# Solving 8 by 8 blocks by substitution on VectorE in the delta rule's triangular inverses

## What is computed

```python
a_mat = jnp.where(strict, jnp.einsum('bnhid,bnhjd->bnhij', kb, kc) * decay, 0.0)
unit_lower = a_mat + jnp.eye(C, dtype=a_mat.dtype)
solve = functools.partial(lax.linalg.triangular_solve, left_side=True, lower=True, unit_diagonal=True)
u = solve(unit_lower, vb)
w = solve(unit_lower, kb * jnp.exp(gc)[..., None])
qk = jnp.where(lower, jnp.einsum('bnhid,bnhjd->bnhij', qc, kc) * decay, 0.0)
```

## Time and profile before

| | |
|---|---|
| median of 3 runs | 2768.18 us (2764.29 to 2771.28) |
| the profiled execution | 2771.26 us |
| its span | 2769.4 us |
| TensorE busy | 2725.2 us, 98% |
| VectorE busy | 1542.8 us, 56% |
| ScalarE busy | 1312.0 us, 47% |
| GpSimd busy | 119.9 us, 4% |
| delta rule's four groups | 360.7 to 466.0 us |

### The profile page before, as it was taken

The page is one execution under the profiler, slowest core; times in us unless marked ns, Lnnn a source line. Parts: engine busy times, 40 slices in busy tenths (PEclk is TensorE's granted clock), DMA queues, the critical chain, the costliest instruction groups (busy, mean ns, idle before and its releaser), DMA issues.

```text
span 2769.4 us, 44546 instructions
## 1 busy us (share of the span) xinstructions
PE 2725.2 (98%) x18174; PEld 2393.0 (86%) x18174; DVE 1542.8 (56%) x2048; ACT 1312.0 (47%) x1798; POOL 119.9 (4%) x167
## 2 busy tenths in 40 slices
PE   8999999999999999999999999999999999999999
PEld 8999998888888888888898997888888888888887
DVE  5655466666555555555544665666665555455454
ACT  4544444555544535445444354335555444354453
POOL 0000043000000000000000000530000000000000
PEclk9999999999999999999999999999999999999999
DMA  7454500543555555555545562004445545555553
GB/s 281 181 184 159 182 33 32 213 172 143 184 201 184 190 191 189 190 183 186 193 175 201 188 220 95 2 2 160 175 140 195 192 173 197 183 191 191 183 194 140
DMA packets 67801, 461.71 MB, mean 167 GB/s; under 512 B 7023, under 2 KB 10223, under 8 KB 13084
## 3 DMA queue, kind: packets, MB, share of 16 engines
q1 hardware_dynamic: 63824, 449.47, 45.3%
q10 hardware_dynamic: 3500, 5.21, 0.6%
q0 software_dynamic: 288, 4.19, 0.4%
HBM read 456.73 MB, written 5.27 MB: 167 GB/s over the span
## 4 chain that ended last, share of the span: by engine, by line
PE 94%; DVE 3%; ACT 2%; issue 1%; DMA 0%; POOL 0%; DVEq 0%; ACTq 0%; POOLq 0%
PE bank L423 17%; PE bank L402 13%; PE bank L404 13%; PE bank L403 13%; PE bank L425 9%; PE bank L446 6%; PE bank L448 6%; PE bank L447 6%; PE bank L1199 1%; PE bank L1172 1%; PE bank L337 1%; PE bank L2477 1%; PE bank L561 0%; PE bank L505 0%; DVE split_lo L353 0%
## 5 line engine op out<-in xcount | busy, mean ns | idle before, releaser
L353 DVE TENSOR_TENSOR split_lo<-raw,split_hi 128x1024 fp32r<-128x1024 f32 x840 | 1019.9, 1224 | 943.1 <-ACT split_hi L346 942.7
L346 ACT ACTIVATE split_hi<-raw 128x1024 fp32r<-128x1024 f32 x840 | 881.4, 1059 | 1137.6 <-PE bank L404 554.9
L423 PE MATMUL bank<-hT,split_hi 128*128 128x512 f32 x2048 | 720.8, 397 | 5.4 <-issue 5.3
L425 PE MATMUL bank<-hT,split_lo 128*128 128x256 f32 x2048 | 574.4, 280 | 0.0
L423 PEld LDWEIGHTS bank<-hT,split_hi 128*128 128x128 f32 x2048 | 385.0, 188 | 93.4 <-DVE split_lo L353 1.1
L402 PE MATMUL bank<-split_hi,u_hi 128*128 128x512 f32 x1152 | 449.8, 390 | 0.0
L404 PE MATMUL bank<-split_hi,u_lo 128*128 128x512 f32 x1152 | 448.5, 389 | 0.0
L403 PE MATMUL bank<-split_lo,u_hi 128*128 128x512 f32 x1152 | 448.4, 389 | 0.0
L425 PEld LDWEIGHTS bank<-hT,split_lo 128*128 128x128 f32 x2048 | 387.4, 189 | 5.7 <-issue 5.6
L446 PE MATMUL bank<-hT,split_hi 128*128 128x256 f32 x1328 | 376.8, 284 | 0.0
L448 PE MATMUL bank<-hT,split_lo 128*128 128x256 f32 x1328 | 375.8, 283 | 0.0
(11 more groups left out here) (471 smaller groups left out, 2266.4 us busy)
## 6 DMA issues: line engine op xcount, KB each, us to landing
raw<-in_stream SPq DMA_DIRECT2D x420, 1024.0 KB, 4.8
work<-in_mem POOLq DMA_DIRECT2D x2, 2048.0 KB, 8.5
bias_rows<-bias_line SPq DMA_DIRECT2D x1, 3072.0 KB, 12.9
x<-in_x SPq DMA_DIRECT2D x1, 2048.0 KB, 9.0
out<-x SPq DMA_DIRECT2D x4, 512.0 KB, 4.9
mwork<-bias_rows ACTq DMA_DIRECT2D x1, 1536.0 KB, 11.2
work<-bias_rows ACTq DMA_DIRECT2D x1, 1536.0 KB, 10.1
rwork<-in_wide ACTq DMA_DIRECT2D x1, 1280.0 KB, 5.9
```

What stands on the lines that cost most here:

```text
L346: nc.scalar.activation(split_hi[:, u % SPLIT], raw[:, b % RAW, (u % 2) * UNIT:(u % 2 + 1) * UNIT], ACT.Copy).then_inc(s_hi, 1)
L353: nc.vector.tensor_tensor(split_lo[:, u % SPLIT], raw[:, b % RAW, (u % 2) * UNIT:(u % 2 + 1) * UNIT], f32(split_hi[:, u % SPLIT]), SUB).th ...
L423: nc.tensor.matmul(out[:, :], lhsT=w_hi[:, cols], rhs=hT[:, k].rearrange("p two s -> p (two s)"), start=k == 0, stop=False)
L425: m = nc.tensor.matmul(out[:, S:2 * S], lhsT=w_lo[:, cols], rhs=hT_hi[:, k, :], start=False, stop=k == KD - 1)
```

## The change

A constant BASE = 3 and TINY = 8. The groups 0 to 3 (delta rule) start at level 3; RWKV's groups at level 1 as before. What stands for levels 0 to 2:

- VectorE, for each direction (dve_inv_blocks): multiply iv_diag with a mask of 8x8 blocks, sum over the blocks to 8 columns, spread these over the unit vectors.
- TensorE (pe_inv_around): one f32 product of 128x512 with a constant matrix, which puts all 8 rows of a block on each of its partitions, in bank 6 (bank 4 for group 0).
- VectorE, both directions together (dve_inv_solve): forward substitution for 8 systems in each partition, two operations a step in six steps after a first one, each waiting for the one before; then for each direction a product that spreads the result to blocks, and a transpose.

The tables DN_PE, DN_ACT and DN_DVE are new: cum, mask and kk of direction a are now made two groups ahead, in the last slot of a group (for group 1 before group 0), blocks and solve of the next group stand in slots 2 and 3 of VectorE. The fillers of slots 20 and 23 go; 14 stand in slots 4 and 8 of group 0 each, 8 in slot 15 of groups 2 and 3. Squares of the output move from VectorE to ScalarE, except for the last group. GpSimd makes three masks a group and direction instead of six; the masks of the low levels are loaded apart, on ScalarE's queue, for RWKV alone.

The diff, cut to its core:

```diff
@@
         def pe_inv_level(pe, group, views, AT, level, between):
             T, Tt, Pm, MT, _ = views
             for d in range(2):
-                pe.wait_ge(iv_t, nth(group, level - 1, d))
+                if level == base_of(group):
+                    pe.wait_ge(iv_tt, iv_tt_first(group, d))
+                    if group % 4:
+                        pe.wait_ge(iv_t, nth(group - 1, MASKS, d))
+                else:
+                    pe.wait_ge(iv_t, nth(group, level - 1, d))
...
+        def dve_inv_blocks(dve, group, views, d):
+
+            T, Tt = views[0][:, d], views[1][:, d]
+            if group >= 2 and d == 0:
+                dve.wait_ge(iv_f, group - 1)
+            dve.wait_ge(iv_a, 2 * group + d + 1)
+            own = const[:, C["blocks"]].unsqueeze(1).broadcast_to([P, 4, HALF])
+            dve_step(nc.vector.tensor_tensor(Tt, iv_diag[:, d], own, MULT))
+            dve_step(nc.vector.reduce_sum(tiny[:, 0, d], blocks_of(Tt).rearrange("p m b c -> p m c b"), AX_X))
...
+            nc.vector.tensor_tensor(blocks_of(T), got.broadcast_to(shape), unit.broadcast_to(shape), MULT).then_inc(iv_blk, 1)
+
+        def pe_inv_around(pe, group, views):
+
+            pe.wait_ge(iv_blk, 2 * group + 2)
+            pe.wait_ge(s_eg, 2 * group + 2)
+            nc.tensor.matmul(rep_bank(group)[:, :], lhsT=const[:, C["around"]],
+                             rhs=views[0].rearrange("p d m n -> p (d m n)"), start=True, stop=True).then_inc(iv_rep, 1)
+
+        def dve_inv_solve(dve, group, views):
...
+            dve.wait_ge(iv_rep, group + 1)
+            nc.vector.tensor_copy(row[:, :, 0:1], unit[:, :, 0:1])
+            dve_step(nc.vector.scalar_tensor_tensor(out=row[:, :, 1:], in0=N[:, :, 0, 1:], scalar=const[:, C["unit_neg"]],
+                                                    in1=unit[:, :, 1:], op0=MULT, op1=ADD))
+            for k in range(1, TINY - 1):
+                left = TINY - 1 - k
+                dve_step(nc.vector.tensor_tensor(part[:, :, 0:left], N[:, :, k, k + 1:],
+                                                 row[:, :, k:k + 1].broadcast_to([P, 8, left]), MULT))
+                dve_step(nc.vector.tensor_tensor(row[:, :, k + 1:], row[:, :, k + 1:], part[:, :, 0:left], SUB))
+            own = const[:, C["blocks"]].rearrange("p (b c) -> p b c", c=TINY).unsqueeze(1).broadcast_to([P, 4, TINY, TINY])
+            flat = lambda v: v.rearrange("p m s -> p (m s)")
+            for d, (solved, turned) in enumerate(((Tt, T), (T, Tt))):
+                nc.vector.tensor_tensor(blocks_of(solved[:, d]), own, tiny[:, 1, d].unsqueeze(2).broadcast_to([P, 4, TINY, TINY]),
+                                        MULT).then_inc(iv_tt, 1)
+                dve.wait_ge(iv_tt, 8 * group + 2 * d + 1)
+                nc.vector.transpose(flat(turned[:, d]), flat(solved[:, d])).then_inc(iv_tt, 1)
...
+            for piece in ("cum", "mask", "kk"):
+                pe_delta_pre(pe, 1, 0, piece)
             for hp in range(DN_GROUPS):
                 def between(slot):
...
+                    if hp == 0 and slot in (4, 8):
+                        pe_fill(bank[0], 14)
+                    if hp + 1 < DN_GROUPS and slot == DN_PE["around"]:
+                        pe_inv_around(pe, hp + 1, dn_inv[(hp + 1) % 2])
+                    if hp >= 2 and slot == 15:
+                        pe_fill(bank[1], 8)
...
-                    if slot in (20, 23):
-                        pe.wait_ge(s_D, min(2 * hp + 4, 2 * DN_GROUPS))
-                        pe_fill(bank[7], 4 if slot == 20 else 5)
...
-        DN_PE = {'tail': (0, 1, 3, 7, 9), 'cum': (0, 13), 'mask': (2, 13), 'kk': (0,), 'kq': (10,)}
-        DN_ACT = {'tail': (0, 1, 3), 'pre': (1, 7), 'diag': (9, 11)}
-        DN_DVE = {'R': 1, 'out': 3, 'squares': 5, 'QKT': (5, 8), 'AT': (7, 9), 'first': (9, 11)}
+        DN_PE = {'tail': (0, 2, 4, 8, 10), 'cum': (15, 2), 'mask': (15, 2), 'kk': (15,), 'kq': (6,), 'around': 8}
+        DN_ACT = {'tail': (0, 1, 3), 'pre': (7, 1), 'diag': (1, 2), 'squares': 4}
+        DN_DVE = {'AT': (0, 1), 'blocks': (2, 2), 'R': 1, 'solve': 3, 'out': 5, 'QKT': (6, 7)}
...
-                    if hp + 1 == DN_GROUPS and 7 <= slot < 7 + AHEAD:
+                    if hp >= 2 and slot == DN_ACT["squares"]:
+                        act_delta_squares(act, hp - 2)
+                    if hp + 1 == DN_GROUPS and slot >= 5:
                         act.wait_ge(s_o, DN_GROUPS - 1)
-                        hi_upto(act, starts["ev_out"][1] + slot - 6)
+                        hi_upto(act, starts["ev_out"][1] + slot - 4)
...
             for d in range(2):
                 lo_sc(5, 1 + d)
-                dve_delta_QKT(dve, 0, d)
+                dve_delta_AT(dve, 0, d)
             for d in range(2):
                 lo_sc(5, 3 + d)
-                dve_delta_AT(dve, 0, d)
+                dve_delta_blocks(dve, 0, d)
             for d in range(2):
-                dve_inv_first(dve, 0, dn_inv[0], d)
+                dve_delta_QKT(dve, 0, d)
+            dve_inv_solve(dve, 0, dn_inv[0])
             take_output(5)
```

More of the change, by code:

```diff
@@ L105 @@
 CONST_COLS = [
-    ("ident", P), ("level", 2 * (LEVELS - 1) * (P // 2)), ("eye", P // 2),
+    ("ident", P), ("level", 2 * (LEVELS - 1 - BASE) * (P // 2)), ("eye", P // 2),
+    ("blocks", P // 2), ("around", P), ("unit", TINY), ("unit_neg", 1),
     ("neg", 2 * P), ("cum_mid", 4 * P), ("causal", 4 * P), ("halves", P), ("ones", 1), ("half_cols", 2),
@@ L1179, in pe_inv_level @@
                 i.then_inc(iv_p, 1)
-                between(4 * level - 4 + d)
+                between(4 * (level - base_of(group)) + d)
             for d in range(2):
@@ L1188, in pe_inv_level @@
                     i.then_inc(iv_q, 1)
-                    between(4 * level - 2 + d)
+                    between(4 * (level - base_of(group)) + 2 + d)
                     continue
-                pe.wait_ge(iv_tt, nth(group, level - 1, d, 0, SMALL))
+                pe.wait_ge(iv_tt, iv_tt_of(group, level - 1, d) if level > base_of(group) else before(group, 8, 12) + 4)
                 for m in range(4):
@@ L1209, in pe_inv @@
                 pe.wait_ge(s_eg, 2)
-            for level in range(1, LEVELS):
+            for level in range(base_of(group), LEVELS):
                 pe_inv_level(pe, group, views, AT, level, between)
@@ L1228, in act_inv @@
                         m.then_inc(iv_f, 1)
-                    between(2 * level - 2 + d)
+                    between(2 * (level - base_of(group)) + d)
         def dve_inv_first(dve, group, views, d):
@@ L1805, in between @@
                 def between(slot):
+                    for d in range(2):
+                        if hp + 1 < DN_GROUPS and slot == DN_DVE["AT"][d]:
+                            dve_delta_AT(dve, hp + 1, d)
+                        if hp + 1 < DN_GROUPS and slot == DN_DVE["blocks"][d]:
+                            dve_delta_blocks(dve, hp + 1, d)
                     if hp and slot == DN_DVE["R"]:
                         dve_delta_R(dve, hp - 1)
+                    if hp + 1 < DN_GROUPS and slot == DN_DVE["solve"]:
+                        dve_inv_solve(dve, hp + 1, dn_inv[(hp + 1) % 2])
                     if hp and slot == DN_DVE["out"]:
                         dve_delta_out(dve, hp - 1)
[L1810 to L1811 removed]
                     for d in range(2):
@@ L2955, in constants @@
         level[:, 1, n_] = pair & (own // size > t_ // size)
-    c[:, at["level"]] = level.reshape(P, -1)
+    low_levels = level[:, :, :BASE]
+    c[:, at["level"]] = level[:, :, BASE:].reshape(P, -1)
     c[:, at["eye"]] = own == t_
+    c[:, at["blocks"]] = own // TINY == t_ // TINY
+    c[:, at["around"]] = s // TINY == t // TINY
+    c[:, at["unit"]] = s % TINY == np.arange(TINY)[None, :]
+    c[:, at["unit_neg"]] = -1.0 * (s % TINY == 0)
     c[:, at["neg"]] = np.where(np.hstack([s <= t, s >= t]), 0.0, NEG)
```

215 lines of the change are left out of this document (142 added, 73 removed).

## The result

| | median, us | runs |
|---|---|---|
| changed kernel | 2777.93 (2774.79 to 2786.2) | 11 |
| kernel before, same chips | 2770.44 (2764.29 to 2774.83) | 11 |
| ratio | 1.0032, 95% interval 1.0023 to 1.0042 | |

The change makes the kernel slower by 0.3%. I had forecast 4 us less, with 2772 as the upper end. The profiled execution took 2780.16 us (span 2778.2), 2.2 above its median.

What follows compares the result with a forecast made beforehand. TensorE, busy for 98% of the span, was taken as the bound. Group 0's start at 366.2 plus four shorter groups gave 458.7 against 466.0, 7.3 us saved, less 3 for one clock fall: 2764 us, range 2754 to 2772.

Steps and rivals of the forecast that it cites:

- a solve: VectorE's copy, 13 dependent operations, two products and transposes per group: 4.8 us, with a bound of 6.1.
- its steps: The solve's 13 small dependent VectorE operations, taken as 0.22 us apart.
- the wait before level 6 in group 0: TensorE waits 2.8 us for VectorE's solve and level 5's subtractions, in group 0 alone.
- groups 1 and 2: Delta rule's middle groups on TensorE: 23.1 and 23.2 us, group 1 down from 28.80.
- the product of pe_inv_around: TensorE's 128x512 f32 product spreading the blocks' rows: 0.96 us, four times.
- RWKV's stage ... 0: One more DMA on ScalarE's queue and waits for long-landed tables cost 0, with 0.5 us as a bound.
- My likeliest case has one fall: One fall of TensorE's granted clock, near group 0's start or its 2.8 us wait, costs 3 us: 4.3 saved.
- two new gaps cost 6 and almost nothing is saved: By the skill's rule on idle gaps, two new TensorE gaps cost 6 us of the 7.3 saved.
- Group 0 starts at 366.2: Delta rule's first group starts on TensorE at 366.2 instead of 360.7 us, 5.5 later, behind VectorE's blocks and solve.
- Group 3 at 20.7 us: Delta rule's last group falls from 26.41 to 20.7 us, fillers (2.2) and ScalarE's weight splits (0.8) included.
- 28 in group 0: 28 filler matmuls in group 0, bringing 7.6 us of TensorE time there.
- solve is the new bound: Rival: slower solve steps on the path; gain gone at 0.30 us a step, 2771 at 0.35; chance 0.15.

Runs made afterwards that it cites:

- b1: Changed kernel with 24 waits (12 instructions) directly ahead of the second feed-forward block's loop; 2764.48 us, 0.9985 of the kernel before.
- d1: Kernel before with 60 waits (30 instructions) at the start of TensorE's program; 2761.65 us, 0.9977 of the kernel before.
- a4: Changed kernel with fillers in group 0's two long waits (8 and 11) and 24 instructions of padding at the start; 2761.37 us, 0.9966 of before.
- c1: a4 with group 1's kk moved inside group 0, 5 instead of 14 fillers behind slot 4, 48 padding instructions; 2756.52 us, 0.9953 of before.
- b4: Changed kernel without the 44 fillers inside the groups, with 8 instructions of padding at the start; 2765.09 us, 0.9987 of before.
- c2: Kernel before with 64 waits (32 instructions) directly ahead of the second feed-forward block's loop; 2767.26 us, 0.9993 of before.

## Why the prediction was wrong

Right, each by a row of the changed kernel: a solve takes 5.3 us in group 0 and 4.8 later (4.8 forecast), its steps 0.21 to 0.24 apart; the wait before level 6 in group 0 2.76 us (2.8); groups 1 and 2 23.3 and 23.5 us (23.1, 23.2); the product of pe_inv_around 1.1 (0.96); RWKV's stage unchanged.

Wrong, in order of size:

1. *"RWKV's stage ... 0", and no term at all for the rest behind the delta rule.* I costed all code past it at nothing, since its instructions are the same. Its place in TensorE's program is not. The loop's turns cost 0.47% of the changed kernel (against b1) and 0.23% of the kernel before (against d1): 13.0 against 6.4 us, so 6.6 us of the difference, most of it. With both loops in good places the two kernels are within 0.1% of each other (b1 against d1). The same missing term hides 0.5 us at ev_out and, cause open, up to 3.4 us in the feed-forward blocks' first turns.
2. *"My likeliest case has one fall".* There were three. The forecast named the right mechanism and two of the places (366 and 389), but the likeliest case took only one of them; the third, in group 3, was not thought of. They missed 10.2 us, where the likeliest case had 3; a part of that passed while TensorE waited anyway. The prediction's other sum, "two new gaps cost 6 and almost nothing is saved", gives 1.3 us saved, and the last tail came 1.4 sooner. That it fits so closely is luck: there were three falls, and items 3 and 4 stand beside them. The cause of the first two, idle time, is shown by a4; that of the third is open.
3. *"Group 0 starts at 366.2".* It started at 368.9. VectorE came to the solve at 360.3 rather than 358.5: it was 0.8 us later already at the split of 346.69 (345.90 before), a split beside GpSimd took 1.75 instead of 1.2, and the blocks took 4.4 us instead of 3.8 (1.9 and 2.5 by the starts), their reduction 0.64 where I had 0.42. Then two of the solve's last steps, 0.50 and 0.44 instead of 0.2, met GpSimd. (The prediction's end of the solve, 363.7, is also 0.2 beyond its own terms, 358.7 + 4.8; it ended at 365.6.)

```profile
355.78 0.95 DVE L1302 TENSOR_TENSOR work<-iv_diag,const 128x256 f32<-128x256 f32 x1
...
356.77 0.64 DVE L1303 TENSOR_REDUCE tiny<-work 128x32 f32<-128x256 f32 x1
...
357.45 0.87 DVE L1308 TENSOR_TENSOR work<-tiny,const 128x256 f32<-128x256 f32 x1
...
362.73 0.50 DVE L1332 TENSOR_TENSOR tiny<-tiny 128x16 f32<-128x16 f32 x1
```

   So mask and cum waited for the first solved block until 364.47 (362.3 forecast), and then ran at half clock.
4. *Group 3 at 20.7 us*: 22.3, with the fall and waits of 0.3 and 0.5 in its level 6, where the four fillers left out had stood. In c1, with the same code and no fall, it took 20.2 (435.60 to 455.75): the sum was right and the clock was missing from it.
5. *"28 in group 0"*: the fillers were in the sum as given. In c1, 9 of them are left out and group 0 takes 24.2 us with kk inside it; I had not asked what they cover.

The rival "solve is the new bound" named the right sign and the wrong mechanism. What decided was in none of them.

## What to carry to other kernels

A difference of 0.3% in a program with a runtime loop is no verdict on a change until the loop's turn-around has been looked at: set the waits marked issue at the loop's first line beside each other, and shift the code by a dozen harmless instructions before you judge. An edit that shortens an engine's work may save nothing where it leaves gaps: here the lowered clock took back up to 3.4 us behind gaps of 2 to 3 us. Count the new gaps first, fill exactly those, and take out fillers that cover nothing. When a chain on a second engine is moved, look for the wait at its new place. And compare the stage's gain with the kernel's: half of c1's 10 us was lost further on.

## What the runs showed of the hardware

- The turn-around of TensorE's loop (1869 instructions by my count) costs from nothing to 3.8 us, by its place in the code alone (d1; the changed kernel).
- A wait for a semaphore that is long satisfied costs TensorE's queue about 0.1 us per instruction of two waits: 100 and 120 of them put its first matmul at 11.78 and 13.95 us.
- In each of the two feed-forward blocks the wide chunks of a turn take some 88.7 or some 90.4 us from first matmul to last, with no wait and at full clock (a pair of matmuls in 0.354 instead of 0.347 us on average in the slow ones). Which turns are slow differs between the traces. But the first turn of the first block takes 88.7 us (680.88 to 769.60 before) in all five traces with the old delta rule and 90.4 (680.90 to 771.32 after) in ten of the eleven with the new one, b4 being the other; the first turn of the second block is fast in four of the five (c2's holds its fall) and slow in nine of the eleven (not in b1 and b4). So the change may cost 3.4 us there. I found no cause, and no run tests it.
- ev_out's first 50 matmuls take 11.1 us with the new delta rule and 10.5 with the old, in every trace; in the changed kernel TensorE waits there for VectorE's split of a weight (0.34 us at 485.72).
